# Four products of activations and norm factor, made by GpSimd instead of VectorE behind the un-normalized chunks

## The reference, cut to what matters

```
def rmsnorm(x, g):
    y = xf * lax.rsqrt(jnp.mean(xf * xf, axis=-1, keepdims=True) + EPS)
    return (y * g.astype(jnp.float32)).astype(x.dtype)

def modulate(h, shift, scale):
    return h * (1 + scale[:, None, :]) + shift[:, None, :]

def swiglu(h, w_in, w_out):
    gu = h @ w_in
    g, u = jnp.split(gu, 2, axis=-1)
    return (jax.nn.silu(g) * u) @ w_out
```

## Time and profile before

| what | us |
|---|---|
| time, median of three runs | 937.09 |
| lowest and highest of them | 935.77, 937.66 |
| the profiled execution, its own time | 928.86 |
| its span | 927.1 |
| TensorE busy | 878.5 |
| VectorE busy | 710.3 |
| ScalarE busy | 468.2 |
| GpSimd busy | 91.0 |

### The profile page before, as it was taken

One profiled execution on the slowest core, in us unless ns is written; L12 is line 12 of the kernel. 1 busy time (PEld: TensorE's weight loads), 2 busy tenths in 40 slices (PEclk: granted clock), 3 DMA queues, 4 the chain that ended last, 5 costly groups with the idle time before them and its releaser, 6 DMA issues.

```text
span 927.1 us, 19318 instructions
## 1 busy us (share of the span) xinstructions
PE 878.5 (95%) x7320; PEld 842.5 (91%) x7320; DVE 710.3 (77%) x1104; ACT 468.2 (51%) x723; POOL 91.0 (10%) x139
## 2 busy tenths in 40 slices
PE   8999998999999988999999979899998979999996
PEld 6888997999999988999999869888998979999995
DVE  4898765999898778788888777678977878866543
ACT  5746654655664457334433455555643754434441
POOL 1022002000001320001012230000000200000010
PEclk9999999999999999899999999999999989999998
DMA  7453345566668974688889947745576347666651
GB/s 254 140 172 98 121 153 204 163 199 185 198 193 294 340 264 139 199 290 297 283 280 324 313 144 245 231 139 183 185 266 222 127 155 249 203 193 204 212 164 46
DMA packets 53334, 191.72 MB, mean 207 GB/s; under 512 B 5920, under 2 KB 6432, under 8 KB 53152
## 3 DMA queue, kind: packets, MB, share of 16 engines
q1 hardware_dynamic: 41760, 149.96, 49.1%
q0 software_dynamic: 10656, 39.33, 12.5%
q10 hardware_dynamic: 864, 1.67, 0.5%
HBM read 189.89 MB, written 1.05 MB: 206 GB/s over the span
## 4 chain that ended last, share of the span: by engine, by line
PE 76%; DVE 14%; ACT 5%; issue 3%; DMA 1%; SPq 0%; DVEq 0%; ACTq 0%
PE ps L388 22%; PE ps L390 22%; PE ps L389 22%; DVE w_lo L1218 5%; ACT w_hi L841 3%; DVE ada_raw L1520 2%; PE ps L460 1%; PE ps L462 1%; PE ps L461 1%; PE ps L496 1%; PE ps L553 1%; DVE rstd_w L1223 1%; DMA X<-x_in 1%; PE ps L527 1%; ACT xn L897 1%
## 5 line engine op out<-in xcount | busy, mean ns | idle before, releaser
L1218 DVE TENSOR_TENSOR w_lo<-raw,w_hi 128x1024 fp32r<-128x1024 f32 x282 | 342.0, 1231 | 114.2 <-ACT w_hi L841 113.8
L388 PE MATMUL ps<-xh,w_hi 128*128 128x256 f32 x1344 | 379.2, 282 | 19.2 <-DVE xl L1277 9.8
L389 PE MATMUL ps<-xl,w_hi 128*128 128x256 f32 x1344 | 374.8, 279 | 0.0
L390 PE MATMUL ps<-xh,w_lo 128*128 128x256 f32 x1344 | 374.7, 279 | 0.0
L841 ACT ACTIVATE w_hi<-raw 128x1024 fp32r<-128x1024 f32 x282 | 287.4, 1052 | 42.7 <-PE ps L390 38.8
L388 PEld LDWEIGHTS ps<-xh,w_hi 128*128 128x128 f32 x1344 | 255.8, 190 | 24.3 <-issue 21.1
L389 PEld LDWEIGHTS ps<-xl,w_hi 128*128 128x128 f32 x1344 | 255.5, 190 | 0.4 <-issue 0.2
L390 PEld LDWEIGHTS ps<-xh,w_lo 128*128 128x128 f32 x1344 | 255.2, 190 | 0.0
L388 PE MATMUL ps<-act_hi,w_hi 128*128 128x256 f32 x528 | 147.2, 279 | 5.0 <-DVE w_lo L1218 4.5
L390 PE MATMUL ps<-act_hi,w_lo 128*128 128x256 f32 x528 | 146.5, 277 | 0.0
L389 PE MATMUL ps<-act_lo,w_hi 128*128 128x256 f32 x528 | 146.5, 277 | 0.0
(11 more groups left out here) (259 smaller groups left out, 1140.8 us busy)
## 6 DMA issues: line engine op xcount, KB each, us to landing
raw<-w SPq DMA_DIRECT2D x282, 512.0 KB, 4.3
ada_raw<-ada_w POOLq DMA_DIRECT2D x72, 512.0 KB, 5.1
X<-x_in SPq DMA_DIRECT2D x4, 256.0 KB, 5.7
bm<-bias_in POOLq DMA_DIRECT2D x1, 1024.0 KB, 6.3
out<-X SPq DMA_DIRECT2D x4, 256.0 KB, 2.2
tab<-tab_in ACTq DMA_DIRECT2D x1, 640.0 KB, 4.2
gmask<-gmask_in ACTq DMA_DIRECT2D x1, 512.0 KB, 5.4
cact<-c_in POOLq DMA_DIRECT2D x1, 512.0 KB, 4.9
```

The source lines that it names most:

```text
L388: pe.matmul(o, lh, rh, start=start, stop=False, skip_group_check=True)
L389: pe.matmul(o, lh, rl, start=False, stop=False, skip_group_check=True)
L390: return pe.matmul(o, ll, rh, start=False, stop=stop, skip_group_check=True)
L1218: v.tensor_tensor(w_lo[:, slot(h), :], raw[:, slot(h), :], w_hi[:, slot(h), :].bitcast(F32), ALU.subtract).then_inc(lo_ready, 1)
```

## The change

The four products are taken out of VectorE's `spread` and put into GpSimd's program, all four behind one wait for the norm factor: for norm 2 after the last sum of squares and before the loads 20 to 42, for norm 5 after the last sum of squares and before the loads 68 to 71. Semaphores and all other work stay.

```diff
+            def pair_mult(n):
+
+                pool.wait_ge(rstd_done, n + 1)
+                for p in range(4):
+                    pool.tensor_tensor(pair(xn, p), pair(X, p), over(rstd[:, :], 2), ALU.mult).then_inc(xt_ready, 1)
...
                 add_gain_squares(k)
                 for n in loads:
                     load_ada(n)
+            pair_mult(2)
             for n in range(20, 43):
                 load_ada(n)
...
             for k in (2, 4, 6):
                 add_squares(4, k, 2)
+            pair_mult(5)
             for n in range(68, 72):
                 load_ada(n)
...
-            def pair_mult(p):
-
-                v.tensor_tensor(pair(xn, p), pair(X, p), over(rstd[:, :], 2), ALU.mult).then_inc(xt_ready, 1)
-
...
                 def spread(j):
                     for p in ((), (0,), (1, 2), ())[j]:
                         pair_lo(m, p)
-                    for p in ((0,), (1, 2), (3,), ())[j]:
-                        pair_mult(p)
```

## The result

The changed kernel is slower by 0.5%: the ratio to before is 1.0051, 95% interval [1.0026, 1.0076], from 20 runs of each (medians 935.62 and 934.01 us). Of 934 us that is 4.8 us, with an interval of 2.4 to 7.1 us. This ratio leaves out runs over 1.5% above the fastest of their kernel, and by that bound 7 of the 20 runs of before go and 2 of the 20 of after; over all 20 of each, the means differ by 3.0 us, with an interval of about 3.2 us to either side. Predicted were 2.8 us. The profiled execution takes 932.66 us, its span is 930.7 us.

A forecast was written before the change was run, and what follows sets the result against it. TensorE was taken as the bound, so only its two waits for `xl` counted. Restarts 1.5 and 1.3 us later, clock 0, make 2.8 us, which on the 937.09 us median gives 939.9 us; range 936.7 to 942.3.

The forecast's parts named there:

- Bound and place: Second block's first FFN chunks, both norms: TensorE's waits for `xl` grow from 5.0 and 4.8 to 6.4 and 6.1 us.
- What is removed is worth 0.2 us per norm: VectorE loses eight products, 5.5 us; only the fourth at each norm is on the path, 0.4 us gained in all.
- Turns: Behind each reciprocal, VectorE and GpSimd alternate on two-SBUF-operand work; VectorE's next `w_lo` comes 1.7 and 1.5 us later.
- first place: First FFN chunks of the second block, at 341 to 372 us; TensorE's restart forecast 1.5 us later.
- second place: The same stage again, at 725 to 756 us; TensorE's restart forecast 1.3 us later.
- rival 1: At both norms GpSimd keeps the turn through all four products: 3.7 us slower, 940.8 us; chance 0.16.
- rival 2: From first product to next `w_lo`, VectorE isn't held on the path: -0.4 us, 936.7 us; chance 0.16.
- the one at 66.03: Trace row: VectorE's 128x256 product took 1.52 us instead of 0.41 beside GpSimd; read as the engines taking turns.
- `act_hi` was mis-sized: First place: this VectorE copy was taken as not held; if held, the estimate would be about 0.25 us more.
- Sum: TensorE's two restarts, 1.5 and 1.3 us later, together 2.8 us slower; the forecast had chance 0.58.
- rival 3: TensorE's half-clock stretch after a restart ends 2 us sooner or later: 937.9 or 941.9 us; chance 0.10.

The follow-up runs named there:

- runs with memsets: The changed kernel with each GpSimd product replaced by a memset, products left out; TensorE restarts 20.28 and 21.21 us after the reciprocal.
- held products: The changed kernel with GpSimd's third and fourth products at each norm made to wait for VectorE; ratio to before 0.9979.
- run with extra products: The kernel before plus four unused GpSimd products behind each norm factor; TensorE restarts 22.80 and 23.07 us after the reciprocal.
- the split version: The kernel before, products on VectorE, with TensorE's one wait for four pairs of `xl` split pair by pair; ratio to before 0.9869.
- wait split, products held back: The changed kernel with TensorE's wait split by pairs and GpSimd's third and fourth products waiting for VectorE; ratio to before 0.9881.

## Why the prediction was right

- *Bound and place.* TensorE's two waits for `xl` were the only places that moved by over 1 us near the change: they went from 5.0 and 4.8 to 6.36 and 5.94 us, where 6.4 and 6.1 were forecast.
- *What is removed is worth 0.2 us per norm.* Shown by the runs with memsets and with held products: 0.20 and 0.10, 0.20 and 0.17 us. VectorE lost 5.5 us of work and the kernel gained at most 0.4.
- *Turns.* Behind the end of the reciprocal, first place, the products were forecast to end at 2.4, 3.7, 6.0 and 7.5 us and ended at 2.41, 3.66, 5.90 and 7.33. In the second place 2.4, 3.7, 5.0 and 7.2 were forecast and 2.41, 3.66, 4.91 and 7.15 measured. GpSimd did not keep the turn between two products while VectorE waited (rival 1), and VectorE was held (against rival 2). The run with extra products shows this as the cause, by itself. The choice of alternation rested on a single row, the one at 66.03.
- *`act_hi` was mis-sized.* I took it as not held. It took 1.26 us instead of 0.29 in the first place. The Trainium skill, SBUF — State Buffer, section "Who interferes with whom", counts a cast in a 2-port mode among what takes the shared pair; by that rule, the trace agrees. The trace shows that this cast is held, and not in which mode it runs. With the 0.25 us that the prediction gave for this case, the next `w_lo` would have been forecast 1.95 us late instead of 1.7, and 1.86 was measured.
- *Sum.* 1.5 + 1.3 us were forecast, 1.66 + 1.11 measured at the restarts, 2.8 either way. In the second place the next `w_lo` came 1.31 us late, not 1.5: the fourth product ended 0.04 us sooner than forecast, `av` only 0.28 us behind it instead of 0.34, and the next `w_lo` 0.71 us behind `av` instead of 0.79. So one place was forecast 0.16 us too low and the other 0.19 us too high. That the sum agrees to 0.03 us is luck; each place is right to 0.2 us.
- *Overlooked.* In the first place TensorE also waited 0.25 us for `cv` of the second chunk, which the turns had made late. It cost nothing, since TensorE was going to wait anyway; in the split version it is what counts.
- *Total.* The timed difference, 4.8 us, is above the 2.8 us, and its interval of 2.4 to 7.1 us holds them; over all runs it is 3.0 us. The other 2 us are not a loss elsewhere, as far as the two profiled executions show. Their spans differ by 3.66 us: 1.41 ahead of the end of norm 2's reciprocal, where the code is the same, 1.66 and 1.11 at the two places, -0.57 between them and 0.05 behind them. The held version, with the same products on GpSimd, shows no loss elsewhere either.
- *Absolute time.* The forecast of 939.9 us was built on a median of three runs, 937.09. Over 20 runs the same kernel has 934.01, and after has 935.62. So the base was not known well enough for a forecast in absolute time. The upper end of the range, 942.3, lies 0.4 above the 941.9 of rival 3, and the prediction doesn't say how it comes about.

## What to carry to other kernels

Before moving an elementwise operation with two SBUF inputs to an idle GpSimd, look up what VectorE does at that moment: a 128x512 product cost a VectorE instruction that met it up to 1.1 us, more than the 0.68 us it saved there. In these runs it was free where VectorE was idle, where it read PSUM (the scaling, 0.69 us either way), or where idle time behind the held instruction took the delay up, and a wait can put it there. And ask first for what TensorE really waits: here a wait for four pairs, of which the last was ready 3.5 us behind the third (370.66 + 0.69 against 366.53 + 1.28 us in VectorE's timeline of before), cost about 12 us over the two norms, with the clock that fell behind it (0.9869 of 932).

## What the runs showed of the hardware that I had not expected

TensorE runs the same loop at one of two paces at a granted clock of 1.00. The same stretch of the program, 180 to 240 us, in the windows of before and of after:

```profile
180.00:240.00 60.00, 60.00 (x532) 60.00 (x531) 53.90 (x101) 35.58 (x57) 0.00 (x0) 1.00 0.63 193
```

```profile
180.00:240.00 60.00, 60.00 (x512) 60.00 (x511) 51.54 (x97) 33.84 (x53) 0.00 (x0) 1.00 0.60 184
```

TensorE is never idle in either and makes 532 products in one and 512 in the other, 4% fewer. VectorE does 4% less as well (101 and 97 instructions), so the products are not merely missing from the record. The change isn't near this stretch. In the windows that I read, the pace stays for a whole loop and differs from loop to loop and from execution to execution: in the last run (wait split, products held back) the stretch from 400 to 460 us has 512 products too, where before has 532. The windows of before and of that run:

```profile
400.00:460.00 60.00, 60.00 (x532) 60.00 (x531) 50.26 (x79) 25.09 (x33) 5.80 (x11) 1.00 0.86 290
```

```profile
400.00:460.00 60.00, 60.00 (x512) 60.00 (x511) 48.02 (x75) 25.07 (x33) 5.80 (x11) 1.00 0.83 282
```

A loop of 100 us at the slower pace costs 4 us, more than the 2.77 us of the two places, and that is why the traces at the two places decide here and single times don't. The code ahead of norm 2 is the same in every kernel here, yet its reciprocal starts at 346.65 us in the second run of the split wait and at 353.59 in the last run. Runs of one kernel scatter by more than one such loop (922 to 942 us for before); that the pace makes up all of it is not shown. What sets the pace is open.
